# Latents' norms made in the input projection, blocks of keys, values and queries in turn, values stored by token

## The chip, the cores and the metric

One core of a Trainium2 chip runs the whole program. The metric is the device time of one execution in microseconds; the kernel before is given as the median of three runs. A profiled execution has its own time.

## The reference, cut to what matters

One residual block on x of 2048 tokens by 1024 channels: a normalised input h is projected by w_in to all inputs of two mixers. What the change touches is the first mixer's latent part:

```python
h = rmsnorm(x, g_pre[l])
proj = h @ w_in[l]
(c_q, c_kv, k_pe, gate_a, hq, hf, hi, gate_b, merge_logits) = jnp.split(proj, split_at, axis=-1)
q = (rmsnorm(c_q, g_q[l]) @ w_uq[l]).reshape(b, s, MLA_HEADS, MLA_QK)
q_nope, q_pe = q[..., :MLA_NOPE], apply_rope(q[..., MLA_NOPE:], cos, sin)
kv = (rmsnorm(c_kv, g_kv[l]) @ w_ukv[l]).reshape(b, s, MLA_HEADS, MLA_NOPE + MLA_V)
k_nope, v = kv[..., :MLA_NOPE], kv[..., MLA_NOPE:]
```

c_q has 768 channels (6 tiles of 128), c_kv has 256 (2 tiles). rmsnorm needs, for each token, the inverse root of the mean of squares over the channels, that is one number per token for c_q and one for c_kv. Behind it come attention over 8 heads, a gated recurrence (the second mixer), and a merge with the output projection. All is float32.

## The kernel before

**Stages in time.** The input projection (to about 700 us), the merge logits with the recurrence (to 1202), the latent projections (1202 to 1443, with the first rows of attention's scores at their end), attention head by head (to about 1980), merge and output. Every float32 product is made of three: each operand is split into a rounded part "hi" and a rest "lo" (`three_products`, lines 74 to 76). ScalarE makes the hi part, VectorE (or POOL) the lo part.

**Input projection** (`input_projection`). The columns of w_in are taken in 17 tiles of 128: first 6 of c_q, 2 of c_kv (`N_LORA` = 8 latent tiles), then others. Each tile is 4 blocks (`NB`) of 512 tokens (`BLK`), 24 matmuls each, in PSUM banks `u * NB + blk` with u the tile's parity. ScalarE evicts a bank to `stage` (`tile_out`) and stores it to projT, channels on the partitions. Three loops `Fori` run over the tiles, on ScalarE and TensorE in step.

**Latent projections** (`latent_projections`). Eight blocks of work in the order `BLOCKS`: keys and values KV of token blocks 0 to 3, then queries Q of 0 to 3. A KV block has 8 evictions: i = 0 to 3 are tiles of keys (two heads each, channels on the partitions), i = 4 to 7 are values (tokens on the partitions); each is 6 matmuls. A Q block has 6 evictions of 18 matmuls: 4 tiles of queries, and from `X_AT` = 4 on two tiles that are rotated (`rotate`). The latent tiles are loaded by `load_c`, and `prepare` squares them (ScalarE, L1309), adds the squares (VectorE, L1401), copies hi (L1312) and makes lo (L1403). Then for each of the 8 norms: `sums` multiplies the added squares by a column of ones on TensorE (L1526), `root` and `inverse` make rstd, `spread` multiplies it out over all partitions (L1537) and `take_spread` evicts that to `rs`. `scale` (VectorE, L1426) multiplies a finished bank by rs into `turned`, `evict` (ScalarE) rounds it into `out`, `split_out` (VectorE) makes the lo part. `BESIDE` is an order written out by hand: which latent tiles ("c") and which of 18 parts of the query weights ("w") ScalarE and VectorE prepare behind which eviction.

**Rings.** Six PSUM banks (`RING`) take the products in turn, `turned` has 3 slots, `out` has 4 (`OUTS`): ScalarE writes a slot only when the store four evictions back has landed. All loads and stores of the stage are issued by SP, in order: the stores (two DMAs each), `load_cs` (16 small DMAs of cosines and sines for one query block), `load_k` (16 small ones for the shared key), `store_k`, and the first head's keys, values and queries (`load_first_keys`, `load_first_queries`, `load_first_shared_key`). Before, `load_cs` stands at the end of a block, `load_k` behind KV 1, the first keys in Q 1.

**Beside the last block** TensorE makes rows 0 to 8 of the first head's scores, one or two rows behind each eviction of Q 3 (`ROWS_BESIDE`, `first_scores`); row 0 waits for `first_k`.

**Values** are stored to vTok, which has a row of 128 floats for each head and token, and are loaded head by head.

## Time and profile before

| | us |
|---|---|
| median of 3 runs | 2369.13 |
| lowest and highest run | 2368.55, 2373.09 |
| the profiled execution, its own time | 2375.12 |
| its span, first to last instruction | 2373.3 |
| TensorE busy (share of the span) | 2220.7 (94%) |
| VectorE busy | 1035.3 (44%) |
| ScalarE busy | 907.4 (38%) |
| POOL busy | 300.3 (13%) |
| mean granted TensorE clock | 0.972 |

PE is TensorE's matmul, PEld its weight load, DVE is VectorE, ACT is ScalarE, SP is SyncE, and a "q" behind an engine's name is its issuing of DMAs. Times in the trace count from the span's start. The granted clock is a share of the full 2.4 GHz; it is either 1 or 0.5 at any instant, and a figure between is a mean. A matmul's duration is longer than the distance to the next one's start, since they overlap: pace is read from the starts. L and a number is a line of the kernel before.

### The profile page before, as it was taken

To read this page: it belongs to the slowest core of one execution; us is meant where nothing else is said; L and a number is where in the kernel's file an instruction comes from. 1 tells how busy PE (TensorE), PEld (TensorE's weight loads), DVE (VectorE), ACT (ScalarE), POOL (GpSimd) and SP (SyncE) were. 2 spreads that over 40 slices of the span, in tenths; PEclk is the share of its full clock that TensorE was granted. 3 is DMA by queue.
4 is the path that set the end of the run, shared out by engine and by line. 5 is a ranking of instruction groups with operands and counts; after the bars stand their busy time and mean duration, and the time that the engine had idled before them with its cause. 6 is when DMAs were issued, how large, how long until landed. Compare 5 with 4: busy or idle time off the path is not lost. (4 is left out here: it accounts for less than half of the span.)

```text
span 2373.3 us, 33277 instructions
## 1 busy us (share of the span) xinstructions
PE 2220.7 (94%) x11664; PEld 1840.5 (78%) x11664; DVE 1035.3 (44%) x1864; ACT 907.4 (38%) x1683; POOL 300.3 (13%) x200
## 2 busy tenths in 40 slices
PE   6999999999979999999967899999999998899998
PEld 5888888778767888888856777788888786778886
DVE  6000000100004555554436746777777676565652
ACT  7111111000114444444335334666566565443441
POOL 1221224032201111111100000000000014200000
PEclk9999999999989999999978998999999999999999
DMA  5222222231212323333257654332123326574751
GB/s 178 85 68 75 75 75 76 80 106 57 94 61 76 97 88 97 97 93 97 71 200 223 197 178 118 69 72 58 40 49 72 72 79 197 171 221 123 219 151 66
DMA packets 213196, 256.41 MB, mean 108 GB/s; under 512 B 39360, under 2 KB 138048, under 8 KB 209600
## 3 DMA queue, kind: packets, MB, share of 16 engines
q1 hardware_dynamic: 188352, 208.21, 30.8%
q10 hardware_dynamic: 23616, 43.00, 4.8%
q0 software_dynamic: 1152, 4.19, 0.5%
q8 instruction: 47, 0.77, 0.1%
q14 instruction: 29, 0.24, 0.0%
HBM read 157.31 MB, written 98.04 MB: 108 GB/s over the span
## 5 line engine op out<-in xcount | busy, mean ns | idle before, releaser
L74 PE MATMUL bankD<-hT_hi,shared_w_hi 128*128 128x512 f32 x512 | 212.3, 415 | 11.7 <-POOLq L703 11.7
L74 PE MATMUL bankA<-hT_hi,shared_w_hi 128*128 128x512 f32 x544 | 212.7, 391 | 0.0
L76 PE MATMUL bankA<-hT_hi,shared_w_lo 128*128 128x512 f32 x544 | 211.9, 390 | 0.0
L75 PE MATMUL bankA<-hT_lo,shared_w_hi 128*128 128x512 f32 x544 | 211.9, 390 | 0.0
L76 PE MATMUL bankD<-hT_hi,shared_w_lo 128*128 128x512 f32 x512 | 201.7, 394 | 0.0
L75 PE MATMUL bankD<-hT_lo,shared_w_hi 128*128 128x512 f32 x512 | 201.0, 392 | 0.0
L1770 DVE TENSOR_REDUCE small_chunk_min<-scores 128x1 f32<-128x512 f32 (+2 forms) x320 | 181.0, 605 | 33.6 <-PE scores L76 18.9
L1790 ACT ACTIVATE probs<-scores,small_least 128x1024 f32<-128x1024 f32 (+2 forms) x192 | 167.3, 872 | 13.2 <-DVE small_least L1777 12.0
L74 PE MATMUL bankA<-wt_hi,hT_hi 128*128 128x512 f32 x384 | 152.6, 397 | 13.3 <-DVE shared_v_raw L392 7.7
L313 ACT ACTIVATE stage<-bankA 128x512 f32<-128x512 f32 x68 | 40.7, 598 | 301.6 <-PE bankA L76 300.1
L75 PE MATMUL bankA<-wt_lo,hT_hi 128*128 128x512 f32 x384 | 150.8, 393 | 0.0
L76 PE MATMUL bankA<-wt_hi,hT_lo 128*128 128x512 f32 x384 | 150.6, 392 | 0.0
L1924 DVE TENSOR_TENSOR pT<-turn_rest,pT 128x512 fp32r<-128x512 f32 (+2 forms) x208 | 126.2, 624 | 53.0 <-ACT pT L1890 53.0
L74 PE MATMUL scores<-k_sb,q_sb 96*128 96x512 f32 (+2 forms) x320 | 127.6, 399 | 16.1 <-ACT probs L1790 14.8
L1890 ACT ACTIVATE pT<-turn_rest 128x512 fp32r<-128x512 f32 (+2 forms) x208 | 109.7, 549 | 67.8 <-PE turn_rest L1976 49.3
L1988 PE MATMUL o_acc<-pT,v_sb 128*128 128x512 f32 (+1 forms) x320 | 125.4, 396 | 4.8 <-DVE pT L1924 3.9
L74 PEld LDWEIGHTS bankD<-hT_hi,shared_w_hi 128*128 128x128 f32 x512 | 97.1, 190 | 31.5 <-issue 12.1
L76 PE MATMUL scores<-k_sb,q_sb 96*128 96x512 f32 (+2 forms) x320 | 120.5, 377 | 0.0
L75 PE MATMUL scores<-k_sb,q_sb 96*128 96x512 f32 (+2 forms) x320 | 119.9, 375 | 0.0
L76 PEld LDWEIGHTS bankA<-hT_hi,shared_w_lo 128*128 128x128 f32 x544 | 102.3, 188 | 21.6
L75 PEld LDWEIGHTS bankA<-hT_lo,shared_w_hi 128*128 128x128 f32 x544 | 102.4, 188 | 21.0
L74 PEld LDWEIGHTS bankA<-hT_hi,shared_w_hi 128*128 128x128 f32 x544 | 102.4, 188 | 20.9
(247 smaller groups left out, 4673.8 us busy)
## 6 DMA issues: line engine op xcount, KB each, us to landing
projT<-stage ACTq DMA_DIRECT2D x68, 256.0 KB, 2.4
shared_w_raw<-in_w_in_dram SPq DMA_DIRECT2D x32, 512.0 KB, 4.4
projT<-d_stage ACTq DMA_DIRECT2D x64, 256.0 KB, 2.4
e_l_in<-projT SPq DMA_DIRECT2D x64, 256.0 KB, 4.8
gateTok<-stage ACTq DMA_DIRECT2D x32, 256.0 KB, 2.0
shared_w_lo<-hgTok SPq DMA_DIRECT2D x16, 512.0 KB, 3.4
knT<-b_out SPq DMA_DIRECT2D x32, 256.0 KB, 2.9
vTok<-b_out SPq DMA_DIRECT2D x32, 256.0 KB, 3.7
```

The source lines that it names most:

```text
L74: pe.matmul(out, a_hi, b_hi, start=first, stop=False)
L75: pe.matmul(out, a_hi, b_lo, start=False, stop=False)
L76: return pe.matmul(out, a_lo, b_hi, start=False, stop=last)
L313: act.activation(stage[:, blk], src, func).then_inc(bank_free, 1)
L1770: dve.tensor_reduce(chunk_min[:, i % 2, c:c + 1], scores[:, s_bank(i, c), 0:width(i, c)], AX.X, ALU.min)\
L1790: act.activation(probs[b][:, r, first * BLK:first * BLK + n], src, ACT.Exp, bias=least[:, i % 2:i % 2 + 1], scale=-1.0, accum_out=sums[:, ...
L1890: act.activation(pT[:, at % RING, 0, r0 * P:], turn[TURN_AT[tile] % TURN_RING][:, r0 * P:], ACT.Copy)\
L1924: dve.tensor_tensor(pT[:, at % RING, 1, r0 * P:], turn[TURN_AT[tile] % TURN_RING][:, r0 * P:], pT[:, at % RING, 0, r0 * P:].bitcast(F32), ...
L1988: pe.matmul(dst, v_sb[u][:, j], pT[:, at % RING, 0, r0 * P:], start=j == 0, stop=False)
```

## The change

In the input projection ScalarE squares each latent bank as it evicts it, VectorE adds the squares over the tiles, and TensorE sums them over the partitions in one run of 32 one-column matmuls between tiles 9 and 10. Root and reciprocal are taken once for all 2048 tokens and both norms; the factors are turned by one transpose and stored as rows (`rsRow`) and as columns (`rsTok`). The loops over tiles are written out where these steps stand. In the latent stage squares, sums, roots and spreads are gone: `load_c` also loads the factors as 128 equal rows. `BLOCKS` becomes KV 0, KV 1, Q 0, KV 2, Q 1, KV 3, Q 2, Q 3, with a new `BESIDE`; `turned` has 5 slots, the last block 4 banks. SP's order changes: `load_cs` behind the fourth store of a query block, `load_k` inside Q 0, the first keys and queries in Q 2. vTok has a row for each token with all heads; a store writes rows of 2 KB, a head's load reads pieces of 512 bytes.

```diff
@@ input_projection: ScalarE
+                def latent_square(n, blk, src):
+                    g, cols = int(n < KQ), slice(blk * BLK, (blk + 1) * BLK)
+                    if n in FIRST_OF_NORM:
+                        dst = c_squares[:, g, cols]
+                    else:
+                        m = SUMMED.index(n) * NB + blk
+                        dst = c_square[:, m % 2]
+                        if m >= 2:
+                            act.wait_ge(c_sq_added, m - 1)
+                    act.activation(dst, src, ACT.Square).then_inc(c_sq_ready, 1)
...
+                for n in range(N_LORA + 2):
+                    tile_out(n, n % 2, ACT.Copy)
+                latent_roots()
+                for n in range(N_LORA + 2, T_HF):
+                    tile_out(n, n % 2, ACT.Copy)
+                latent_rows_out()
@@ VectorE
+                        dve.tensor_tensor(c_squares[:, g, cols], c_squares[:, g, cols], c_square[:, m % 2], ALU.add)\
+                           .then_inc(c_sq_added, 1)
@@ TensorE
+                def latent_sums():
+                    pe.wait_ge(const_set, 2)
+                    pe.wait_ge(c_sq_added, len(SUMMED) * NB)
+                    pe.wait_ge(bank_free, N_LORA * NB + (8 + B_NORM + 1))
+                    for g in range(2):
+                        for t in range(TT):
+                            last = pe.matmul(bank[:, B_NORM, g * TT + t:g * TT + t + 1], c_squares[:, g, t * P:(t + 1) * P], ones[:],
+                                             start=True, stop=True)
+                    last.then_inc(c_sums_done, 1)
...
+                latent_sums()
+                tile_products(0, N_LORA + 2, (c_std_ready, 2))
+                tile_products(1, N_LORA + 3)
+                latent_row()
+                tile_products(0, N_LORA + 4, (c_row_ready, 1))
@@ latent_projections
-    RING, OUTS, TURNED = 6, 4, 3
+    RING, OUTS, TURNED = 6, 4, 5
+    BLOCKS = ((KV, 0), (KV, 1), (Q, 0), (KV, 2), (Q, 1), (KV, 3), (Q, 2), (Q, 3))
-            return e % RING if e < E_LAST else (0, 1, B_SUMS)[(e - E_LAST) % 3]
+            return e % RING if e < E_LAST else (0, 1, 6, 7)[(e - E_LAST) % 4]
+        for i in range(2):
+            beside(KV, 0, i, ("c", KV, 1, i))
+        for i in range(6):
+            beside(KV, 0, 2 + i, ("w", 2 * i), ("w", 2 * i + 1))
+        for i in range(3):
+            beside(KV, 1, i, ("w", 12 + 2 * i), ("w", 13 + 2 * i))
         for i in range(4):
+            beside(KV, 1, 3 + i, ("c", Q, 0, i))
+        beside(KV, 1, 7, ("c", Q, 0, 4), ("c", Q, 0, 5))
+        for blk in (0, 1):
+            for i in range(2):
+                beside(Q, blk, 1 + i, ("c", KV, blk + 2, i))
+            for i in range(3):
+                beside(Q, blk, 3 + i, ("c", Q, blk + 1, i))
+                beside(KV, blk + 2, i, ("c", Q, blk + 1, 3 + i))
+        beside(Q, 2, 1, ("c", Q, 3, 0), ("c", Q, 3, 1))
         for i in range(4):
+            beside(Q, 2, 2 + i, ("c", Q, 3, 2 + i))
@@ SP
+                sp.dma_start(rs[:, g, blk % 2], rsRow[g:g + 1, block_cols(blk)].to_broadcast([P, BLK])).then_inc(c_in[blk % 2][g], 16)
-                        dma = sp.dma_start(vTok[part * 4:(part + 1) * 4, :, blk * TPB + i - V_AT, :].rearrange("h p n -> p h n"),
-                                           src.rearrange("p (h n) -> p h n", n=2 * VD))
+                        dma = sp.dma_start(vTok[blk * TPB + i - V_AT, :, part * BLK:(part + 1) * BLK], src)
...
+                    if (g, blk, i) == (Q, 0, 1):
+                        load_c(1, Q)
+                        load_c_again(3, KV)
+                    if g == Q and blk in (1, 2) and i == 0:
+                        load_c_again(blk + 1, Q)
                     store(g, blk, i)
                     if (g, blk, i) == (Q, 0, 2):
+                        load_k()
+                    if (g, blk, i) == (KV, 2, 3):
                         store_k(0)
+                    if (g, blk, i) == (Q, 1, 3):
+                        store_k(1)
+                    if g == Q and blk + 1 < NB and i == X_AT - 1:
+                        sp.wait_ge(cs_ready, blk * 2 + 2)
+                        load_cs(blk + 1)
+                    if (g, blk, i) == (Q, 2, 1):
...
                         attend.load_first_keys(sp)
+                        for of in range(2):
+                            attend.load_first_queries(sp, of)
...
+                    if (g, blk, i) == (Q, 2, X_AT):
                         sp.wait_ge(k_stored, 16 * 4 * NB)
                         attend.load_first_shared_key(sp)
@@ attention
-                             vTok[ds(i * 2 + u, 1)].rearrange("o p t n -> (o p) t n")).then_inc(head_in[u], 16)
+                             vTok[:, :, ds(i * (2 * P) + u * P, P)].rearrange("t p n -> p t n")).then_inc(head_in[u], 16)
```

## Rows read from the trace of the kernel before

**Rows 1.** Windows: from:to and length; each engine's busy us (instructions); clock, DMA share, GB/s

```profile
60.00:411.00 351.00, 351.00 (x1550) 290.73 (x1549) 0.33 (x2) 41.44 (x67) 97.03 (x44) 1.00 0.25 76
1202.00:1220.00 18.00, 0.40 (x2) 0.00 (x0) 4.56 (x8) 5.13 (x11) 1.65 (x7) 0.59 0.67 227
1220.00:1262.00 42.00, 33.52 (x137) 27.59 (x138) 23.50 (x44) 20.71 (x40) 0.00 (x0) 0.83 0.76 251
1262.00:1304.00 42.00, 34.33 (x137) 27.66 (x138) 26.69 (x47) 22.60 (x44) 0.00 (x0) 0.82 0.74 225
...
1398.00:1443.00 45.00, 42.04 (x183) 34.49 (x184) 21.77 (x46) 13.81 (x29) 0.10 (x1) 0.88 0.32 107
```

**Rows 2.** Waits, 1202 to 1446: who, for whom, total us, times, longest

```profile
PE bankB L1526 <- DVE b_acc L1401: 18.6, 5, 5.0
PE bankB L74 <- DVE b_c_lo L1403: 18.1, 1, 18.1
ACT b_wk_hi L1295 <- DMA small_ident<-in_ident_dram: 12.7, 1, 12.7
...
ACT b_out L1337 <- DMA knT<-b_out: 6.5, 6, 2.0
...
PE scores L74 <- ACT probs L1790: 3.0, 2, 2.5
PE bankB L1537 <- DVE b_rstd L1409: 2.9, 2, 2.0
...
PE bankB L74 <- issue: 2.8, 1, 2.8
...
PE bankB L1526 <- ACT b_std L1318: 1.4, 1, 1.4
```

**Rows 3.** Timeline of PE: start, us, what, count, idleness before it and its releaser

```profile
1238.87 1.52 PE L1526 MATMUL bankB<-b_ones,b_acc 128*128 128x1 f32 x8 [2.94 <-DVE b_acc L1401]
...
1240.82 0.63 PE L75 MATMUL bankB<-b_c_lo,b_wk_hi 128*128 128x512 f32 x1
1241.24 0.63 PE L76 MATMUL bankB<-b_c_hi,b_wk_lo 128*128 128x512 f32 x1
...
1246.26 0.40 PE L76 MATMUL bankB<-b_c_hi,b_wk_lo 128*128 128x512 f32 x1
1246.49 0.40 PE L74 MATMUL bankB<-b_c_hi,b_wk_hi 128*128 128x512 f32 x1
...
1329.98 0.95 PE L1526 MATMUL bankB<-b_ones,b_acc 128*128 128x1 f32 x8
1330.79 0.49 PE L74 MATMUL bankB<-b_c_hi,b_wq_hi 128*128 128x512 f32 x1
```

**Rows 4.** Timeline of DVE in KV 0

```profile
1239.33 0.69 DVE L1438 TENSOR_TENSOR b_out<-b_turned,b_out 128x512 fp32r<-128x512 f32 x1
1239.94 0.74 DVE L1432 SCALAR_TENSOR_TENSOR b_out<-bankB,b_rstd,b_out 128x512 fp32r<-128x512 f32 x1
1240.60 1.00 DVE L1390 SCALAR_TENSOR_TENSOR b_wq_lo<-b_wq_raw,b_gain,b_wq_hi 128x512 fp32r<-128x512 f32 x2
1241.52 0.74 DVE L1432 SCALAR_TENSOR_TENSOR b_out<-bankB,b_rstd,b_out 128x512 fp32r<-128x512 f32 x1
```

**Rows 5.** Timeline of SP: start, us until the last of them was issued

```profile
1248.11 9.67 SPq L1196 DMA_DIRECT2D b_cos_sin<-in_rope_dram  x16
```

**Rows 6.** Chain of work that ended last, between Q 1 and Q 2: start, us, what

```profile
1360.36 0.69 DVE b_cross L1453
...
1364.39 1.05 PE bankB L1526 x8
```

**Rows 7.** DMA issues, 1202 to 1446: count, KB each, median us from issue to landing

```profile
knT<-b_out SPq DMA_DIRECT2D x32, 256.0 KB, 2.9
vTok<-b_out SPq DMA_DIRECT2D x32, 256.0 KB, 3.7
...
k_sb<-kpT SPq DMA_DIRECT2D x2, 256.0 KB, 10.2
```

More of the change, by code:

```diff
@@ L148, in input_projection @@
         lb_exp = sem("lb_exp")
+        c_sq_ready = sem("c_sq_ready")
+        c_sq_added = sem("c_sq_added")
+        c_sums_done = sem("c_sums_done")
+        c_std_ready = sem("c_std_ready")
+        c_rstd_step = sem("c_rstd_step")
+        c_row_turned = sem("c_row_turned")
+        c_row_ready = sem("c_row_ready")
+        c_stored = sem("c_stored")
+        FIRST_OF_NORM = (KQ, 0)
+        SUMMED = [n for n in range(N_LORA) if n not in FIRST_OF_NORM]
+        B_NORM = NB - 1
         N_TILES = T_PE + 1
@@ L236, in _ @@
                 pool.memset(eps[:], EPS).then_inc(const_set, 1)
+                pool.memset(ones[:], 1.0).then_inc(const_set, 1)
                 def split_tile(u, n, arrived):
@@ L319, in _ @@
                     act.sem_inc(s, 16)
-                with act.Fori(0, T_HF // 2) as i:
-                    for u in range(2):
-                        tile_out(i * 2 + u, u, ACT.Copy)
+                for n in range(N_LORA + 2):
[4 more added lines that the diff above has]
+                latent_rows_out()
                 with act.Fori(0, (T_PE - T_HF) // 2) as i:
@@ L434, in tile_products @@
                         pe.wait_ge(bank_free, n * NB + (blk + 1))
+                        if norm_read is not None and blk == B_NORM:
+                            pe.wait_ge(*norm_read)
                         cols = slice(blk * BLK, (blk + 1) * BLK)
@@ L441, in _ @@
                 tile_products(1, 1)
-                with pe.Fori(1, T_PE // 2) as i:
+                with pe.Fori(1, N_LORA // 2 + 1) as i:
+                    for u in range(2):
+                        tile_products(u, i * 2 + u)
+                latent_sums()
[3 more added lines that the diff above has]
+                tile_products(0, N_LORA + 4, (c_row_ready, 1))
+                tile_products(1, N_LORA + 5)
+                with pe.Fori(N_LORA // 2 + 3, T_PE // 2) as i:
                     for u in range(2):
@@ L1504, in vector @@
                             split_weights(N_WKV + job[1])
-                    if (g, blk, i) == (KV, 2, 5):
-                        inverse(Q, 0)
-                    if g == Q and blk == 0 and 0 < i < X_AT:
-                        (turn_shared_key, split_shared_key)[(i - 1) % 2]((i - 1) // 2)
-                if (g, blk) == (Q, 0):
-                    split_shared_key(1)
-                if g == KV and blk + 1 < NB:
-                    inverse(KV, blk + 1)
-                if g == Q and blk < NB - 1:
-                    inverse(Q, blk + 1)
-        def tensor(pe, attend):
-            pe.wait_ge(const_in, 48)
-            pe.wait_ge(const_set, 2)
-            def sums(g, blk):
-                n = NORM_AT[g, blk]
-                pe.wait_ge(sq_added, PREPARED_AT[g, blk, len(TILES[g]) - 1] + 1)
-                if n > 0:
-                    pe.wait_ge(std_ready, n)
-                for t in range(TPB):
-                    last = pe.matmul(bank[:, B_SUMS, n * TPB + t:n * TPB + t + 1], acc[:, g, t * P:(t + 1) * P], ones[:],
-                                     start=True, stop=True)
-                last.then_inc(sums_done, 1)
-            def spread(g, blk):
-                n = NORM_AT[g, blk]
-                pe.wait_ge(rstd_ready, n + 1)
-                if n > 0:
-                    pe.wait_ge(rs_ready, n)
-                for t in range(TPB):
-                    at = blk * TPB + t
-                    last = pe.matmul(bank[:, B_SPREAD, t * P:(t + 1) * P], rstd[:, g, at:at + 1].to_broadcast([P, P]), ident[:],
-                                     start=True, stop=True)
-                last.then_inc(spread_done, 1)
+                    for y, (of, at, _) in enumerate(KEY_TURNS):
+                        if (g, blk) == (of, at) and i in (0, 2):
+                            (turn_shared_key, split_shared_key)[i // 2](y)
+        def tensor(pe, attend):
+            pe.wait_ge(const_in, 64)
             def bank_read(e):
-                g = KV if e < Q_FIRST else Q
-                blk, i = (e - number(g, 0, 0)) // EVICTIONS[g], (e - number(g, 0, 0)) % EVICTIONS[g]
+                g, blk, i = NUMBERS[e]
                 if g == KV and i >= V_AT:
@@ L1581, in tensor @@
                     last.then_inc(prod_done, 1)
-                    if (g, blk, i) in SUMS_AFTER:
-                        sums(*SUMS_AFTER[g, blk, i])
-                    if (g, blk, i) in SPREAD_AFTER:
-                        spread(*SPREAD_AFTER[g, blk, i])
                     if (g, blk, i) == (Q, NB - 1, 0):
@@ L2488, in hybrid_mla_hgrn2_gated_merge @@
         small = Small(nc, ctx)
-        latent_sems, latent = latent_projections(nc, small, projT, g_q, g_kv, w_uq, w_ukv, rope, ident, qnT, qpT, knT, kpT, vTok)
+        latent_sems, latent = latent_projections(nc, small, projT, rsRow, rsTok, g_q, g_kv, w_uq, w_ukv, rope, ident, qnT, qpT, knT, kpT, vTok)
         attend_sems, attend = attention(nc, small, latent, qnT, qpT, knT, kpT, vTok, ident, oA)
```

239 lines of the change are left out of this document (88 added, 151 removed).

## The prediction

> **What bounds the kernel now.** I read the windows by stage first [rows 1]. The reader is to see that TensorE is busy for all of the 351 us of the input projection's tiles at the full clock, and that the latent stage (1202 to 1443 us) is the one stretch where it is not: 18 us with nothing to multiply, then two stretches of 42 us with about 34 busy and a granted clock of 0.82 to 0.83; at its end, beside the first scores, the clock is 0.88. So whatever is added to TensorE in the projection lengthens the kernel by its whole length, and whatever is taken from its path in the latent stage shortens it.
>
> The waits of the latent stage come second [rows 2]. TensorE's largest, after the head's 18.1, is 18.6 us over five waits of the sums (L1526) for the last added square (L1401); with b_rstd, b_std, issue and scores the waits behind the head are 18.6 + 1.4 + 2.9 + 2.8 + 3.0 = 28.7 us. The timeline of TensorE shows what follows a wait [rows 3]: after 2.94 us of idleness the wide matmuls start 0.42 us apart (the level of 1.2 GHz) and only from 1246.26 on are they 0.23 us apart (2.4 GHz). Some twelve to thirteen matmuls at half speed cost 0.2 us each, 2.4 us for one wait.
>
> The ledger of 1202.4 to 1443.0, 240.6 us: head 18.1; 624 matmuls of 512 columns (192 for keys and values, 432 for queries) at 0.227, 141.5; nine rows of first scores, 17,280 columns at that pace and nine masks, 9.5; eight groups of sums at 0.81 (1329.98 to 1330.79) [rows 3] and eight of spreads, taken at the same price, 12.9; waits 28.7. The 29.9 left are half-clock time. Sums and spreads, waits and half clock together are 71.5 us; the change attacks these.
>
> **The projection.** 32 squares on ScalarE (busy 41 of the 351 us, 67 evictions of 0.6 [rows 1]), 24 additions on VectorE (idle there) and two small stores are covered by 351 us of products; uncovered, the squares alone would be 32 x 0.6 = 19 us. The roots' table load on ScalarE is covered as well: it evicts four banks behind. TensorE's part is not covered: 32 sums are eight groups of 0.81 = 6.5 us, one transpose 0.2. They now stand in one row. Nothing in the trace shows 6.5 us of one-column matmuls in a row, so the clock behind them is open: at best the full clock stays (6.7 us in all); at worst they run at half clock (a group after a wait lasts 1.52 in its row against 0.95 [rows 3]; twice the pace is 0.8 more for each of the eight, +7) and the next twelve matmuls too (+2.4): 16 us. A single group at the full clock is followed by the full clock [rows 3], a row of eight is between; I take full clock inside and one stretch of half clock after, 6.7 + 2.4 = 9.1 us.
>
> The Trainium skill (TensorE: Matmul & The Clock Gate, Back-to-back issue gap) puts the floor of narrow matmuls at about 25 ns from start to start; by that the 64 records would take 1.6 us and not 6.5, and the net gain below would be 22.8 us and not 17.9. The trace disagrees: eight records in 0.81 us are 101 ns each.
>
> **The head of the latent stage.** The first matmul waits for ident's DMA [rows 2], and two more DMAs now stand ahead of it (rs of block 0, 256 KB, and rstd): two issues of 0.45 and some data, +1.0. Against it, VectorE no longer adds a square and ScalarE no longer takes two before c_lo is ready, -0.8. Net 0; the first product stays at 1220.5 (call it 0 below).
>
> **The stage by blocks.** Steps on VectorE start 0.60 apart for 128x512, 0.66 for values, 0.92 for two weight parts [rows 4]; a hand-over to ScalarE and back (one eviction and one copy of 0.6 each, of which VectorE covers about 0.7) costs about 0.5 beyond that.
>
> *Keys and values 0 and 1.* VectorE: 16 steps for eight key tiles, 9.6; eight values, 5.3; eight latent tiles, 4.8; 18 weight parts, 7.9: 27.6. Plus 2.6 for the first product at half clock and eleven hand-overs, 5.5: queries 0 can start at 35.9 (TensorE, with 21.8 of work, waits some 11 us for the last c tile). The queue says the same: 12 MB (16 evictions of 512 KB and the loads left) at 251/0.76 = 330 GB/s [rows 1] are 36 us. Before, these blocks took 41.3, with six weight parts and six latent tiles less done.
>
> *Queries 0, values 2.* 24.5 + 10.9 of work, 2.4 half clock. SP is in order: behind the store of query tile 2 stand 16 loads of the key tables, then 16 of the cosines; 16 such issues took 9.7 us [rows 5] with waits for room among them, and I draw them at 8. So tiles 3 to 5 are stored up to 10 us late; ScalarE has a ring of four slots and stands still at the third key tile of block 2, and with it the c tiles of queries 1. TensorE waits 3.4 us at queries 1, banks cost another 1.4: 42.6.
>
> *Queries 1, values 3.* Same, without the key tables: 24.5 + 10.9 + 2.4 + 1.9 wait = 39.7.
>
> *Queries 2.* 24.5 + 1.4 (half clock), then TensorE waits for the last tile of queries 3. Before, its idleness at this place ran from 1360.3 to 1364.4, over the rotation's four steps, ScalarE's square and one addition, and behind the sums the next product began at about 1365.4 [rows 6]. The square and sum go (-1.9), but the last tile is now prepared one eviction later (+2.5): 5.6. Together 31.5.
>
> *Queries 3 and first scores.* 44.6 before; the spread goes (-0.8). The shared key is now loaded behind the fifth store of queries 2, which waits behind 16 cosine loads; I get its landing at 14 us after the end of queries 2, and TensorE wants it at 12: +2. 45.8.
>
> Sum 35.9 + 42.6 + 39.7 + 31.5 + 45.8 = 195.5, against 222.5 before (1443.0 - 1220.5): 27.0 us gained. Bounds: if ScalarE and SP never hold VectorE, blocks 0 and 1 take 27.6 + 2.6, queries 1 wait 3 less and the key isn't late: 38. If each of the four table loads takes 9.7 (4 x 1.7) [rows 5], and the shared key lands as late as it did, 10.2 us from issue [rows 7] where I draw 4 (+6): 14.
>
> **Values in rows of 2 KB.** The stores go from 512 B pieces, 3.7 us to landing, to what knT has, 2.9 [rows 7]; 0.8 us less for 16 value stores, and it is in the ring of four. I leave it inside the 35.9, since VectorE is level there; ScalarE's 6.5 us of waits for stores [rows 2] are its whole worth. The loads of v go the other way, 8 KB pieces to 512 B: eight loads of 1 MB, each issued by the code a head ahead of its use, so hidden behind a head of attention; uncovered each would be longer by the same 0.8 us in 256 KB, 3.2 us, 26 us in all.
>
> The Trainium skill (DMA: Bandwidth & Descriptors, Specifications) names 512 B as the least size at line rate; by that neither side would change. The two landings of [rows 7] disagree.
>
> POOL's part is a memset less; the output stage's start is unchanged.
>
> **Net.** 27.0 - 9.1 = 17.9 us. The profiled execution (2375.12 us, span 2373.3) would be 2357.2; the median of the runs is 6 us under it, so 2369.1 - 17.9 = 2351.2 us. A measurement here tells from about 0.2% (4.7 us).
>
> **Rivals.**
> *A. The sums halve the clock (0.15).* 16 us in the projection instead of 9: 27 - 16 = 11, 2358 us. For it: half clock comes readily in this kernel [rows 3]. Against: where it does, the engine stood idle before, and the sums leave it no idleness.
> *B. The handing-over costs less than I draw (0.18).* Blocks 0 and 1 at VectorE's busy time, no late key: 38 - 9 = 29, 2340 us. For it: TensorE may run six banks ahead. Against: SP's order.
> *C. The waits only move (0.10).* The 18.6 us of waits on squares return as waits for c tiles at each change of block, with the half clock; only spreads (6.4) and what the projection gives back (-9.1 + 6.5) are left: about 2365 to 2369. For it: at the end of each query block TensorE already waits for rotation and hand-over. Against: two of the three query blocks are now followed by keys whose tiles are long ready.
> *D. Slower (0.07).* SP's queue holds the stores: stores, 16 cosine loads and 16 key loads come in the middle of a block, and the ring of four stops ScalarE. Priced above at 3.4, 1.9 and 2; it decides once SP is 6 us later than drawn in each of the three query blocks, which takes the 18 us; at 10 us later, 2381 us. For it: the length of one such load [rows 5]. Against: the same loads were issued in the stage before, and no wait of TensorE there was for a store.
>
> **How the numbers follow.** My sum has 0.50. Its own range, from the bounds 14 and 38 less 9.1, narrowed: 2345 to 2360. For eight in ten I go from B to the near end of C: 2338 to 2366. Faster: my sum 0.50, A 0.14, B 0.18 and 0.01 of C, 0.83; same: most of C and 0.01 of A, 0.10; slower 0.07.
>
> **What would show it.** Right: the projection's sums as 64 records in about 6.5 us; no bankB group of one or 128 columns left in the latent stage; VectorE without gaps through blocks 0 and 1; SP holding tiles 3 to 5 of queries 0 behind cosine loads; the first transposes of attention 27 us sooner after the first bankB product. Wrong: granted clock under 1 for over 4 us behind the sums; TensorE's waits in the stage still above 25 us; attention's heads longer because v arrives late.

## The result: slower by 0.4%, where 0.8% faster was forecast

| | before | after |
|---|---|---|
| median, us (6 runs each) | 2369.32 | 2379.08 |
| lowest and highest | 2367.58, 2373.09 | 2374.55, 2381.64 |
| ratio, 95% interval | 1 | 1.0038 (1.0025 to 1.0051) |
| profiled execution, its span | 2375.12, 2373.3 | 2374.55, 2372.7 |
| first product of the latent stage | 1220.53 | 1229.61 |
| first transposes of attention | 1443.03 | 1445.10 |
| between the two | 222.5 | 215.5 |

2351.2 us was forecast, in a range of 2338 to 2366. The two traces make the difference look smaller than the medians do: the profiled execution of before was slower than its six runs, that of after the fastest of its own. Up to the first transposes they show +9.1 (first product) and -7.0 (between the two), that is +2.1 us.

The windows of the kernel after, as in [rows 1], from the input projection, from the sums within it, from the first two blocks of the latent stage and from its end:

```profile
60.00:411.00 351.00, 351.00 (x1562) 292.27 (x1561) 20.03 (x28) 55.58 (x98) 96.91 (x44) 0.99 0.24 74
258.00:269.00 11.00, 11.00 (x67) 10.94 (x66) 0.00 (x0) 0.69 (x2) 5.11 (x2) 0.66 0.25 73
...
1229.00:1268.00 39.00, 25.20 (x96) 19.27 (x96) 29.55 (x53) 22.04 (x44) 0.00 (x0) 0.81 0.85 292
...
1385.00:1405.00 20.00, 5.72 (x19) 4.35 (x19) 0.72 (x2) 0.63 (x1) 0.00 (x0) 0.67 0.74 203
```

The clock of the projection's window is 0.99 where it was 1.00, and 0.66 over the sums. In the last window TensorE works 5.7 of 20 us, VectorE and ScalarE under 1 us each: all three wait for one thing. The waits of 1202 to 1446, beside [rows 2], name it:

```profile
PE bankB L74 <- DVE b_c_lo L1433: 43.7, 5, 17.9
...
PE scores L74 <- DMA k_sb<-kpT: 14.2, 1, 14.2
...
ACT b_out L1385 <- DMA knT<-b_out: 8.8, 8, 2.0
ACT b_out L1390 <- DMA qnT<-b_out: 8.3, 1, 8.3
...
ACT b_c_hi L1376 <- DMA b_rs<-rsRow: 6.9, 3, 5.6
```

TensorE's waits for sums and spreads are gone. In their place are four waits for latent tiles at the changes of block, 43.7 - 17.9 (the head) = 25.8 us, and one of 14.2 us for the shared key. TensorE's timeline at the two places where the time was lost:

```profile
258.25 10.62 PE L503 MATMUL bankA<-ones,c_squares 128*128 128x1 f32 x64
268.73 0.77 PE L74 MATMUL bankA<-hT_hi,shared_w_hi 128*128 128x512 f32 x1
...
271.01 0.63 PE L76 MATMUL bankA<-hT_hi,shared_w_lo 128*128 128x512 f32 x1
...
1385.08 0.80 PE L74 MATMUL bankB<-b_c_hi,b_wq_hi 128*128 128x512 f32 x1 [5.88 <-DVE b_c_lo L1433]
...
1404.98 0.44 PE L74 MATMUL scores<-k_sb,q_sb 96*128 96x128 f32 x1 [14.20 <-DMA k_sb<-kpT]
```

The 64 records of the sums (the profile has two for each of the 32) take 10.5 us, 0.164 each where a short group had 0.101 [rows 3], and seven products behind them still start 0.40 to 0.57 apart, not 0.23. The chain of work that ended last shows why the key is late (start, us, what). SPq is an issue by SP: lines 1703 to 1706 load a small constant, the first keys and values, 1715 and 1717 the first queries, 1273 the cosines, 1710 the shared key; 1304 and 1306 store queries:

```profile
1361.92 8.00 DMA b_rs<-rsRow
1369.94 0.64 ACT b_c_hi L1376
...
1374.17 0.56 SPq L1703
...
1376.70 0.59 SPq L1706
1377.33 5.24 SPq L1715
...
1387.41 0.58 SPq L1717
1389.44 0.46 SPq L1304
1389.94 0.47 SPq L1304
1390.45 0.62 SPq L1273
...
1398.48 0.51 SPq L1306
1399.50 0.45 SPq L1710
1400.00 4.71 DMA k_sb<-kpT
1404.98 0.44 PE scores L74
```

For 43 us, from 1361.9 to 1405.0, the end of the kernel hangs on a transfer and on SP's queue, hardly on an engine that computes. Behind the first keys SP issues two blocks of queries (12 loads, 1377.3 to 1388.5; the first of these issues took 5.24 us, right behind the 1 MB load of the values), then stores, 16 cosine loads (1390.5 to 1398.4), one more store, and only then the key, which needs nothing that was made in the last 30 us.

### The profile page after: what moved, and what is told of

The parts are those of the page before. It is cut to its first block and busy times, and to the rows that moved or that the text cites. A ratio compares the mean times of both kernels' runs of the same rounds, so it can differ in the third digit from the quotient of the medians.

```text
span 2372.7 us, 32911 instructions
## 1 busy us (share of the span) xinstructions
PE 2205.5 (93%) x11601; PEld 1827.8 (77%) x11601; DVE 1037.6 (44%) x1858; ACT 898.9 (38%) x1668; POOL 300.2 (13%) x199
## 5 line engine op out<-in xcount | busy, mean ns | idle before, releaser
L74 PEld LDWEIGHTS bankD<-hT_hi,shared_w_hi 128*128 128x128 f32 x512 | 96.9, 189 | 31.5 <-issue 12.2
L76 PEld LDWEIGHTS bankD<-hT_hi,shared_w_lo 128*128 128x128 f32 x512 | 96.8, 189 | 21.8
```

Of the source, the lines that this page charges most:

```text
L74: pe.matmul(out, a_hi, b_hi, start=first, stop=False)
L76: return pe.matmul(out, a_lo, b_hi, start=False, stop=last)
```

## The experiments

Each run has one trace and is timed against the kernel before on its own chip. "Stage" is the time from the first product of the latent stage to the first transposes of attention: it can be read to 0.1 us, but two traces of one kernel differ by up to 4. The medians have a scatter of their own: from the first transposes to the end the traces take 922.8 us (e15_pool) to 933.6 (e5_cos), though no edit but e6_values' touches what runs there.

| run | what differs from the changed kernel | first product | stage | median | ratio (95%) |
|---|---|---|---|---|---|
| e0_after | nothing | 1233.6 | 214.6 | 2376.9 | 1.0024 (1.0010 to 1.0039) |
| e13_before | the kernel before | 1220.2 | 223.1 | 2369.1 | 0.9988 (0.9976 to 1.0000) |
| e1_key | key early | 1232.2 | 201.8 | 2363.2 | 0.9958 (0.9943 to 0.9973) |
| e1_again | the same | 1232.5 | 197.8 | 2361.2 | 0.9963 (0.9949 to 0.9976) |
| e2_sums | sums in groups | 1227.8 | 215.6 | 2372.6 | 0.9997 (0.9982 to 1.0011) |
| e3_order | old order of blocks | 1230.1 | 211.9 | 2374.8 | 1.0011 (0.9997 to 1.0025) |
| e8_order2 | old order, old place of scaled table | 1232.2 | 205.1 | 2368.1 | 0.9994 (0.9985 to 1.0004) |
| e4_cload | key early, tiles of Q 3 loaded early | 1231.8 | 203.7 | 2367.2 | 0.9987 (0.9975 to 0.9999) |
| e5_cos | key early, cosines later | 1232.5 | 199.7 | 2363.4 | 0.9972 (0.9961 to 0.9982) |
| e6_values | key early, values in 512 B | 1232.2 | 201.1 | 2364.7 | 0.9986 (0.9977 to 0.9994) |
| e7_tiles | key early, tiles a block ahead | 1231.7 | 209.4 | 2370.9 | 1.0003 (0.9993 to 1.0013) |
| e9_all | e7 and sums in groups | 1228.5 | 209.6 | 2364.8 | 0.9971 (0.9961 to 0.9982) |
| e10_outs | key early, ring of five | 1229.4 | 200.0 | 2355.6 | 0.9931 (0.9915 to 0.9947) |
| e12_spo | e7, SP's order changed | 1233.8 | 206.6 | 2368.9 | 0.9989 (0.9976 to 1.0001) |
| e14_tiles_outs | e7, ring of five | 1229.8 | 202.0 | 2360.9 | 0.9953 (0.9937 to 0.9969) |
| e11_three | key, groups, ring of five | 1226.7 | 196.8 | 2348.8 | 0.9903 (0.9882 to 0.9924) |
| e15_pool | e11, latent reloads by POOL | 1227.6 | 196.7 | 2349.0 | 0.9907 (0.9884 to 0.9930) |
| e16_pool_tiles | e15, tiles a block ahead | 1228.2 | 193.7 | 2345.4 | 0.9890 (0.9867 to 0.9913) |

**Both kernels once more.**

> The changed kernel once more, nothing edited. Its first profile had a span of 2372.7 us and the lowest time of its six runs (2374.55; median 2379.08), the profile of the kernel before the highest (2375.12; median 2369.1), so the two traces show about 10 us less of the difference than the medians. Theory 1: the difference is real and lies in stretches at half clock that come and go; then a second profile has a span nearer 2377 to 2379, with the same waits in the latent stage (c tiles 43.7 us, shared key 14.2 us, each within 1.5) and the surplus in granted clock under 1, spread over attention and the output. Theory 2: the trace was typical and the medians differ by the chip; then this run's ratio to before is under 1.001. Ratio expected: 1.002 to 1.005.

> The kernel before once more, nothing edited, for a second trace of it. Its first profiled execution took 2375.12 us, above all of its six runs. If that lay in stages that the change doesn't touch, the first product of the latent stage stands at 1220 to 1221 again and the stage at 222 to 223 us; if the projection and recurrence vary by some us from run to run, the first product stands elsewhere by 2 us or more. Ratio to before 0.999 to 1.001.

The second traces hold the shares: first product at 1220.2 (before) and 1233.6 (after), stage 223.1 and 214.6. Over all thirteen traces with the sums in one row the first product starts at 1229.4 to 1233.8. So the change costs 9 to 13 us ahead of the stage and gives 7 to 9 back in it. The second trace of the changed kernel has the same waits (43.9 us for tiles and the head, 14.0 for the key). The kernel before read 0.9988 against itself, so a tenth of a per cent between two ratios means nothing.

**The shared key.**

```diff
                         attend.load_first_keys(sp)
+                        sp.wait_ge(k_stored, 16 * 4 * NB)
+                        attend.load_first_shared_key(sp)
                         for of in range(2):
                             attend.load_first_queries(sp, of)
...
-                    if (g, blk, i) == (Q, 2, X_AT):
-                        sp.wait_ge(k_stored, 16 * 4 * NB)
-                        attend.load_first_shared_key(sp)
```

> Only the load of the shared key moves: from behind the fifth store of queries 2 to just behind the first keys (behind the second store of queries 2), ahead of the sixteen cosine loads. Theory 1 (the key was simply issued too late): TensorE's wait of 14.2 us for it at 1391 goes, and with it the dozen half-clock matmuls behind it (2.4 us), so 14 to 17 us less than the changed kernel: ratio to before about 0.997 to 0.998. Theory 2 (TensorE would have waited in any case, for the first keys, the first queries or a bank, which come from the same queue): the wait stands under another name, 6 us gained or less, ratio 1.001 to 1.002.

> The changed kernel with the shared key loaded early, once more, to compare the next three against on the same chip. The two calls before put variants of it at ratios from 0.9958 (itself) to 0.9986; expected here 0.995 to 0.998, and from the first product of the latent stage to the first transposes of attention 200 to 203 us again (201.8 the first time).

13.8 us less than e0_after by the medians, both timed on one chip, and 12.8 to 16.8 less by the stages. The wait is gone, and only in the first of its two traces do 2.4 us stand under another name (first queries, at 1397). Two moved lines make the change a gain.

**The sums.** Between the products of tile 9 and not behind it:

```diff
                             last = three_products(pe, bank[:, u * NB + blk], (w_hi[:, u, k], w_lo[:, u, k]),
                                                   (hT_hi[:, k, cols], hT_lo[:, k, cols]), k == 0, k == KD - 1)
+                            if sums and blk >= 2 and k % 2 == 0:
+                                some_sums((blk - 2) * 4 + k // 2)
...
-                latent_sums()
```

> Only the 32 sums of the projection are placed otherwise: eight groups of four between the products of tile 9 (its blocks 2 and 3), with the tile taken out of its loop, where the change has all 32 in one row behind the tile. Same work. Theory 1 (a long row of one-column matmuls itself brings TensorE to 1.2 GHz: 64 records in 10.5 us, 0.164 each, and seven products at half clock behind): small groups stay at 2.4 GHz, 0.81 us each, 6.5 in all with no half-clock products: 5.4 us less than the changed kernel, granted clock 1.00 from 230 to 290 us. Theory 2 (0.16 us is what such a matmul costs in this place, by its operands, whatever stands around it): 10 us again and no gain, or more with the switches between banks. Ratio to before by theory 1 about 1.0017, by theory 2 1.004.

```profile
249.25 0.95 PE L504 MATMUL bankA<-ones,c_squares 128*128 128x1 f32 x8
250.06 0.49 PE L74 MATMUL bankA<-hT_hi,shared_w_hi 128*128 128x512 f32 x1
...
251.54 0.95 PE L504 MATMUL bankA<-ones,c_squares 128*128 128x1 f32 x8
```

A group takes 0.81 us and the full clock follows; the granted clock of 230 to 290 us is 1.00 and not 0.91. 4.3 us less by medians (5.4 forecast), and the first product comes at 1226.7 to 1228.5 in the five traces that have it, still 6 to 8 us behind the kernel before: 6.5 of that are the groups themselves. The row of sums itself brought the engine to the level of 1.2 GHz, though it was never idle (busy 11.0 of the 11 us at a clock of 0.66).

**The order of blocks.** All of the change but the order, first with the scaled table where the change has it, then where it was:

```diff
-    BLOCKS = ((KV, 0), (KV, 1), (Q, 0), (KV, 2), (Q, 1), (KV, 3), (Q, 2), (Q, 3))
+    BLOCKS = tuple((KV, blk) for blk in range(NB)) + tuple((Q, blk) for blk in range(NB))
...
-                    if g == Q and i == 1:
-                        scaled_table(blk)
                     if g == Q and i == X_AT:
                         split_out(Q, blk, X_AT - 1)
+                        scaled_table(blk)
```

> The changed kernel with the old order of blocks: keys and values 0 to 3, then queries 0 to 3, with the old table of what is prepared beside which eviction and the old places of the loads (cosines behind a block, key tables behind keys 1, first keys in queries 1, shared key behind the fifth store of queries 1). Factors from the projection, rows of 2 KB and five slots of turned stay. Theory 1 (the factors are worth what the forecast said and the new order eats it): from the first product of the stage to the first transposes of attention 190 to 205 us, against 215.5 in the changed kernel and 222.5 before; ratio to before 0.990 to 0.996. Theory 2 (the waits for squares only turn into waits for latent tiles in either order, because VectorE and ScalarE hand over to each other at the same pace): 210 to 216 us, ratio 0.999 to 1.004.

> The old order of blocks with the old places of loads, as tried before, and now also the old place of the scaled table (VectorE multiplies cosines by the factors behind the fourth query tile, not behind the second). In the run before VectorE stood 5.1 us at this step for the cosines of queries 2, and TensorE waited 8.8 us at each of queries 2 and 3. Theory 1 (the table's new place, with the loads behind the block, was what held it): the two waits fall to about 5 us, 8 to 12 us less than then with the half clock: from the first product to the first transposes about 201 us, ratio to before 0.996 to 0.998. Theory 2: tiles are late for the rotation's sake; still 8 us each, ratio 1.000 to 1.002.

The first showed a trap of my edit: the scaled table had stayed in its new place while its cosine loads had gone back to theirs. VectorE's timeline in queries 2 of e3:

```profile
1386.08 1.29 DVE L1445 TENSOR_TENSOR b_cs_q<-b_cos_sin,b_rs 128x512 f32<-128x512 f32 x2 [5.10 <-DMA b_cos_sin<-in_rope_dram]
```

With the table back in its place TensorE's wait at queries 2 fell from 8.8 to 4.1 us, but the one at queries 3 only from 8.8 to 8.1: theory 1 holds for one of the two. The stage is 205.1, against 197.8 to 201.8 for the new order with the key early. By the stages the new order is worth 3 to 7 us. Everything else in the change (factors from the projection, rows of 2 KB, slots and banks) is worth 18 of the old order's 223; no run parts these, though three slots of turned in place of five cost nothing that e10_outs shows.

**Load, cosines, values.** On top of the early key, each alone:

```diff
# e4_cload
-                    if g == Q and blk in (1, 2) and i == 0:
-                        load_c_again(blk + 1, Q)
+                    if (g, blk, i) == (Q, 1, 0):
+                        load_c_again(2, Q)
+                    if (g, blk, i) == (Q, 1, X_AT):
+                        load_c_again(3, Q)
# e5_cos
-                    if g == Q and blk + 1 < NB and i == X_AT - 1:
+                    if g == Q and blk + 1 < NB and i == (X_AT + 1, X_AT + 1, X_AT - 1)[blk]:
```

> With the shared key loaded early (as in the run before), and one more move: the load of the latent tiles and factors of queries 3 is issued before the fifth store of queries 1, and not before the first store of queries 2, behind all stores of keys and values 3. In the run before ScalarE stood 8.2 us in queries 2 until this load had landed (issued at 1364.4, landed at 1373.9), and TensorE waited 8.0 us for the last tile at queries 3. Theory 1 (the late load makes the long wait): ScalarE's 8.2 goes, and TensorE's wait at queries 3 falls to the 5 us that rotation and hand-over need, or less; 3 to 5 us less than with the key alone, ratio to before about 0.994. Theory 2 (the wait is the rotation's, behind which the last two tiles are prepared, wherever the load stands): 7 to 8 us of wait stay, ratio 0.9955 to 0.9965.

> With the shared key loaded early, and in queries 0 and 1 the sixteen cosine loads issued behind the block's last store and not behind the fourth, so that no store of a query block waits behind them (keys and values follow, so the tables are in time). The forecast put 3.4 us of wait at queries 1 and 1.9 at queries 2 down to SP's queue, and rival D called it the bound. If that is right: TensorE's waits at queries 1 and 2 (3.1 and 2.7 us in the run before) and their half-clock products shrink, 3 to 8 us less than with the key alone, ratio 0.9925 to 0.9945. If the waits come from the hand-over between ScalarE and VectorE in keys 2 and 3 and not from stores: no change, ratio 0.9955 to 0.9965.

> With the shared key loaded early, and values stored and loaded as in the kernel before (a row of 512 bytes for each head and token; a head's load in pieces of 8 KB). If the rows of 2 KB are worth nothing, as the forecast has it: within 0.1% of the run with the key alone (ratio 0.995 to 0.9968). If the shorter issue and landing of the stores matter, because ScalarE waits for stores in the ring of four: 2 to 4 us more. If the loads of 512 B pieces cost attention: 2 to 5 us less, seen in the heads' lengths between 1460 and 1975 us.

e4 missed both ways. ScalarE's 8.2 us went, and the wait at queries 3 fell to 5.9, but the one at queries 2 rose from 2.7 to 8.2. ScalarE's timeline in keys 3 tells why:

```profile
1357.75 0.63 ACT L1391 ACTIVATE b_out<-b_turned 128x512 fp32r<-128x512 f32 x1 [6.93 <-DMA qpT<-b_out]
```

The store of the rotated queries, issued at 1349.8, now stands right behind the load of 1.5 MB issued at 1348.8, and ScalarE, four evictions on, waits for its slot. e5 changed nothing, so the cosine loads don't hold queries 1 and 2: the forecast's 3.4 and 1.9 us were put on the wrong cause. Those waits, 3.4 and 2.7 us in e0, 3.1 and 2.7 in both traces of e1, are 2.9 and 2.7 here. e10 below says it again: there ScalarE's stops for stores, 24 to 26 us with the early key alone, are down to 3.7, and the same two waits are 2.9 and 2.7. e6 has a ratio 0.0014 above e5's, timed on one chip, with overlapping intervals, and 0.0023 to 0.0028 above the early key's own on other chips; its stage is the same. The 2 KB rows are worth between nothing and 0.3%, and these runs don't settle it. A head's load of v lands after 14.4 us (early key) instead of 13.6 (e6), hidden as forecast, and the forecast's 3.2 us for it was too much.

**Tiles a block ahead, SP's order, the ring, another queue.** Six tiles of the next query block beside evictions 0 to 3, and what was then changed about it:

```diff
# e7_tiles
+            beside(Q, blk, 0, ("c", Q, blk + 1, 0), ("c", Q, blk + 1, 1))
+            for i in range(2):
+                beside(Q, blk, 1 + i, ("c", KV, blk + 2, i), ("c", Q, blk + 1, 2 + i))
+            beside(Q, blk, 3, ("c", Q, blk + 1, 4), ("c", Q, blk + 1, 5))
...
+                    if g == Q and blk in (0, 1) and i == X_AT:
+                        load_c_again(blk + 2, Q)
# e10_outs, e14_tiles_outs
-    RING, OUTS, TURNED = 6, 4, 5
+    RING, OUTS, TURNED = 6, 5, 3
# e15_pool, e16_pool_tiles
+            for g, blk in ((KV, 2), (Q, 1), (KV, 3), (Q, 2), (Q, 3)):
...
+                pool.dma_start(c_lo[blk % 2][:, first:end].bitcast(F32),
+                               projT[first:end, :, block_cols(blk)].rearrange("k p n -> p k n")).then_inc(c_again[g, blk], 16)
```

> With the shared key loaded early, and all six latent tiles of a query block prepared beside evictions 0 to 3 of the query block before (two at a time), so that none is left behind a rotation or inside keys and values; their loads are issued a block earlier (before the fifth store of the query block two before; those of queries 1 in keys 1). The same work, other places. Theory 1 (TensorE waits at queries 1, 2 and 3, 3.1 + 2.7 + 8.0 us with some 24 half-clock products, since the last tiles stand behind what ScalarE and VectorE do late in a block): all three waits go or stay under 1 us, about 14 + 4 us: from the first product to the first transposes 182 to 188 us, ratio 0.988 to 0.991. Theory 2 (the stage is held by stores: a load of 1.5 MB in front of a store lengthens it, ScalarE stands in its ring of four, and TensorE runs out of banks instead of tiles): the stops of ScalarE for a store stay at 20 us or more and TensorE's waits come back on banks, 196 us or more, ratio over 0.994.

> With the shared key loaded early, a fifth slot in out, the ring out of which the stores go, and three slots in turned instead of five (as in the kernel before; the memory holds no more). If ScalarE's stops for a store (some 27 us in the stage) are what makes tiles late, a fifth slot takes 5 to 10 us of them off ScalarE and 2 to 5 us off TensorE's waits. If they lie where TensorE has banks ahead and the tiles are late for their place in the order: TensorE's waits unchanged within 1.5 us, stage 200 to 203 us.

> The shared key early, the tiles a block ahead, and the sums in eight groups of four between products: the three places together. By theory 1 they add: first product of the latent stage 4 to 5 us earlier than with the row of sums (1227 to 1228 and not 1232), and the stage as with the tiles ahead alone; ratio 0.986 to 0.989, some 30 us under the kernel before. By theory 2 0.992 or more.

> The tiles a block ahead, as tried before (209.4 us from the first product to the first transposes; ScalarE stopped 28.2 us for the stores of the rotated queries), with nothing but SP's order changed: the key tables behind the first query tile, the cosine loads behind the third, second and first store of queries 0, 1, 2 (as soon as VectorE has scaled the table before), the loads of latent tiles behind a block's last store, the queries of block 1 behind the fourth store of queries 2. Theory 1 (the stores of the rotated queries were late because SP issued 16 cosine loads and a 1.5 MB load ahead of them): ScalarE's 28 us fall under 10, TensorE's waits for banks (14.7 us) go, stage 185 to 196 us, ratio 0.988 to 0.993. Theory 2 (it is the ring of four or the DMA engines' rate): still 20 us or more of stops, stage over 203 us, ratio over 0.997.

> The tiles a block ahead with SP's order as first tried, but the ring out with five slots and turned with three. Theory 2 of the run above (the ring): stops of ScalarE for stores fall from 48 us to under 25, stage 190 to 200 us. Theory 1 (SP's order holds the stores 10 us, longer than one more slot covers): ScalarE stops at the rotated queries as before or 5 us less, stage 203 to 209 us.

> Three small moves on the changed kernel: shared key early, sums in eight groups between products, five slots in out and three in turned. Alone on the changed kernel or on the key, they gave 13.8, 4.3 and 5.6 us by medians. If they add: 23 to 24 us under the changed kernel, 2352 to 2354 us, ratio 0.990 to 0.992. If the third was a chance of the chip (its trace shows the stage no shorter): ratio 0.993 to 0.995.

> The three small moves together (key early, sums in groups, five slots in out), and the five later loads of latent tiles with their factors (those of keys 2 and 3 and of queries 1, 2 and 3) are issued by POOL, which has nothing else to do in this stage, on its own queue and as soon as their buffers are free, instead of by SP between its stores. If stores are late because they stand in one queue behind loads of 1.5 MB, and tiles late because the loads stand behind stores: ScalarE's 6.8 us stop at queries 2 for the load goes, TensorE's wait at queries 3 falls from 6.6 to 5 or less, 2 to 5 us less than the three moves alone, ratio 0.988 to 0.9895. If the transfers' bytes hold each other up whatever queue they are in: no gain, 0.990 to 0.992.

> The same with the tiles of a query block prepared in the query block before, which with SP's loads brought ScalarE 29 to 49 us of stops for stores and TensorE 10 to 15 us of waits for banks. If one queue's order was the cause: stops under 12 us, no wait of TensorE at queries 1, 2 and 3, stage 180 to 190 us, ratio 0.983 to 0.987. If it is the engines' rate, with cosines and stores still on SP: stops over 20 us, waits for banks of 7 us or more, stage over 195 us, ratio 0.991 or more.

e7 was my best guess and cost 8 to 12 us. TensorE's waits for tiles at queries 1, 2 and 3 did go, and others came. Its waits of 1268 to 1446, ScalarE's and TensorE's:

```profile
ACT b_out L1389 <- DMA qpT<-b_out: 28.2, 4, 14.1
ACT b_out L1389 <- DMA qnT<-b_out: 10.3, 1, 10.3
ACT b_out L1384 <- DMA knT<-b_out: 7.7, 9, 2.3
...
PE bankB L74 <- DVE b_out L1456: 14.7, 2, 8.5
```

ScalarE stands 49 us for stores (28.2 + 10.3 + 7.7, and 3.0 for values), against 22 to 24 with the early key alone, and TensorE runs out of banks. e12 changes only SP's order. The total stays at 47 us and the names change; TensorE's wait for the first queries, whose loads the same edit moved back, grows from 7.0 to 12.7 us:

```profile
ACT b_out L1385 <- DMA knT<-b_out: 19.5, 10, 7.4
ACT b_out L1390 <- DMA qnT<-b_out: 18.7, 4, 14.5
ACT b_out L1390 <- DMA qpT<-b_out: 8.6, 4, 3.7
```

The rotated queries' stores now cost 8.6 us and not 28.2, and those of the keys, now behind the load of 1.5 MB, 19.5 and not 7.7. A fifth slot (e14, with e7's order of SP) takes the total to 29 us and the stage from 209.4 to 202.0:

```profile
ACT b_out L1389 <- DMA qpT<-b_out: 24.0, 2, 12.7
ACT b_out L1384 <- DMA knT<-b_out: 3.7, 6, 0.8
ACT b_out L1384 <- DMA qpT<-b_out: 1.4, 2, 0.7
```

and with the loads on POOL's queue (e16) it is 23 us, while the wait for banks falls from 9.9 us to 3.5 and none is left at queries 1:

```profile
ACT b_out L1405 <- DMA qpT<-b_out: 12.1, 2, 8.9
ACT b_out L1400 <- DMA knT<-b_out: 4.2, 6, 0.9
ACT b_out L1405 <- DMA qnT<-b_out: 2.9, 2, 1.9
ACT b_out L1405 <- DMA knT<-b_out: 1.9, 1, 1.9
...
PE bankB L74 <- DVE b_out L1472: 3.5, 1, 3.5
PE scores L74 <- DMA q_sb<-qpT: 7.6, 1, 7.6
```

What the 23 us are, e16's trace tells. Its longest stop, 8.9 us, ends when this store lands (a line of SP's timeline, then the chain of work):

```profile
1337.07 9.22 SPq L1282 DMA_DIRECT2D b_cos_sin<-in_rope_dram  x16
...
1346.33 0.42 SPq L1315
...
1346.80 2.98 DMA qpT<-b_out
1349.80 0.64 ACT b_out L1405
```

Sixteen cosine loads still stand ahead of the store in SP's queue, 9.2 us of issues. In e14 they stand there too, the load of 1.5 MB behind them, and the rotated queries' stores of that place then took 7.7 us from issue to landing, against 3.1 in e16. So the stops are mostly one thing: stores in one in-order queue, behind cosine loads (7 to 9 us of issues) and behind a large load (some 5 us of landing), with a ring that is short for them. They follow the load to whichever store is behind it and shrink with a slot; e16, which differs from e14 also in the sums and in when the loads are issued, has them smaller again. The rate of the engines isn't needed to explain what is left, and neither of e16's two forecasts came out. The Trainium skill (DMA: Bandwidth & Descriptors, Queues, rings and completion order) says that each DMA engine takes a queue's descriptors in ring order and goes round-robin between queues; the landings of 7.7 and 3.1 us agree.

What e7's own idea is worth isn't shown even then: stage 193.7 against 196.7 in e15, 3 us, within the 4 by which two traces of one kernel differ, and far from the 180 to 190 expected. Three waits for tiles (11.5 us in e15) went, and 3.5 us for a bank and 7.6 for the first queries came.

e15 against e11 gained nothing, where 2 to 5 us were expected: ScalarE no longer waits for any load, and TensorE still waits 5.9 us at queries 3 (6.6 in e11), where [rows 6] has 4.0 from the rotation's second half on. It looks like the rotation and the hand-over behind it, now with two tiles left behind it instead of one, as theory 2 of e4 had it; earlier loads buy next to nothing there.

e10 took ScalarE's stops for stores from 24 to 26 us down to 3.7, and TensorE hardly noticed: its waits for tiles are 2 us shorter, and the stage, 200.0, is no shorter than the early key's 197.8 and 201.8. Its 5.6 us of median lie where its edit changes nothing: the first product comes 3 us earlier, the last stretch is 2 us shorter. In this order of tiles the ring of four was no bound; it became one in e7.

Measured by medians the three small edits gave 13.8 + 4.3 + 5.6 = 23.7. e11_three, with all of them, is 2348.8 us: 28 us under the changed kernel's 2376.9 on another chip, 22 under before on its own. **e16_pool_tiles, 2345.4 us, ratio 0.989, is the shortest of all**; it is 3.7 us below e15 and their intervals overlap.

## Why the prediction was wrong, step by step

- **What bounds the kernel**: right. What was gained or lost lay on TensorE's path in the two places named; behind the first transposes the changed kernel's two traces take 928 us, those of the kernel before 930.
- **The projection**: half right. Cover for squares, additions and roots held (ScalarE busy 55.6 instead of 41.4 us, TensorE 351 of 351). The sums were sized at 6.5 at full clock with 2.4 behind, 9.1; they took 10.5 with 1.4 behind, 11.9. Rival A named the mechanism; its "against", that the sums leave no idleness, was the wrong reason: the clock fell without any.
- **The head**: right (17.9 for 18.1), the step called 0.
- **Keys and values 0 and 1** 38.8 for 35.9 (its own terms add to 35.7, and 18 weight parts at 0.92 for two are 8.3 and not 7.9), **queries 0 with values 2** 43.4 for 42.6, **queries 1 with values 3** 41.1 for 39.7, **queries 2** 32.3 for 31.5: sizes right to 6 us in all, though the causes drawn for queries 1 and 2 were not (e5, e10), so that the near hit there is luck.
- **Queries 3 and the first scores**: the step that failed, 60.0 for 45.8. The prediction said "I get its landing at 14 us after the end of queries 2, and TensorE wants it at 12: +2". TensorE wanted it 11.6 us after; it landed 25.5 after. Of SP's work ahead of the key the forecast names the fifth store and the cosines, which took the 8 us that it drew for them, and leaves out the first keys, values and twelve query loads that the same edit moved into queries 2 (14.3 us, 1374.2 to 1388.5). The block came 14.2 us over its forecast, and two moved lines took 13 to 17 us off the kernel; missed were 24 to 28 in all (from -17.9 to +5.7 and +9.8 by the two comparisons). Of the rest 6 are the blocks above, 3 the sums, and the others lie within the scatter of the traces.
- **Rival D**, slower through SP's queue, had 0.07, and slower it came. The queue was the right place and the waiter the wrong one: D had the ring of four stop ScalarE behind loads. ScalarE did stand 24 to 25 us for stores, 6.5 to 6.9 before, but without these stops (e10) the stage was no shorter; only with tiles a block ahead was a slot worth 7 us of it (e14 against e7). What decided was the key in the same queue. **Rival C** was also partly right: 18.6 us of waits for squares became 25.8 for tiles. The forecast's own sum already held 21.9 of them (11, 3.4, 1.9 and 5.6; measured 12.2, 4.3, 3.3 and 5.9).
- **The shared key's wait alone turns the sign**: without it the change is 0.4% faster (e1_key, e1_again), 2361 to 2363 us, inside the range of the forecast. With the sums in groups as well it would be near 2357 to 2359, worked out, not run. Of the signs named, the sums' 10.5 us in place of 6.5 and the waits above 25 us (25.8 and 14.2) showed the forecast wrong; longer heads didn't come.

## What to carry to other kernels

When an edit moves DMA issues in a queue that works in order, write the queue out around the last waiter and count every issue ahead of it (0.45 to 0.65 us each here, and 5.24 for one behind a load of 1 MB): two loads of 256 KB, whose data had lain ready for over 50 us (stored by 1342), were issued 13 us after the last moment at which they would have been in time (1386), and that cost 13 to 17 us where the whole change without it is worth 8 to 11. Look at stores behind a large load, or behind many small ones: here a load of 1.5 MB ahead of them took their landing from 3.1 to 7.7 us and sixteen small loads held their issue by 7 to 9. Whether such a stop costs anything is a second question; ask whether the engine that bounds the kernel waits longer (it didn't until e7). And before preparing operands earlier, ask what their transfer will stand in front of.

## What the runs showed of the hardware

A row of 64 one-column records brought TensorE from 2.4 to 1.2 GHz without an idle instant, and groups of eight between wide products did not (0.164 and 0.101 us a record). After the same wait of 2.72 us the clock fell in some traces and not in others. The kernel with the early key in its second trace, and the one with five slots, both at the first products of queries 2:

```profile
1354.52 0.50 PE L74 MATMUL bankB<-b_c_hi,b_wq_hi 128*128 128x512 f32 x1 [2.72 <-DVE b_c_lo L1432]
1354.85 0.40 PE L75 MATMUL bankB<-b_c_lo,b_wq_hi 128*128 128x512 f32 x1
1355.09 0.40 PE L76 MATMUL bankB<-b_c_hi,b_wq_lo 128*128 128x512 f32 x1
```

```profile
1349.22 0.50 PE L74 MATMUL bankB<-b_c_hi,b_wq_hi 128*128 128x512 f32 x1 [2.72 <-DVE b_c_lo L1432]
...
1350.29 0.63 PE L75 MATMUL bankB<-b_c_lo,b_wq_hi 128*128 128x512 f32 x1
1350.72 0.63 PE L76 MATMUL bankB<-b_c_hi,b_wq_lo 128*128 128x512 f32 x1
```

That alone makes blocks of 24.8 and of 26.4 us of the same 108 products. The changed kernel's own two traces have one of each (24.8 in e0_after behind 2.72 us, 26.4 in the first trace behind 3.27), which is part of why two traces of one kernel differ.

Left open: where e10's 5.6 us of median come from, since its stage is no shorter than the early key's; what sets the largest wait that is left in the stage, 12.2 us ahead of queries 0 (11.9 to 13.8 in every run with the new order); and what the rows of 2 KB are worth.
